# The last down-projection tile in parts of 384 and 128 tokens in place of two of 256

## What is computed

```
x = x + 0.5 * swiglu(rms_norm(x, ffn1_norm), ffn1_gate, ffn1_up, ffn1_down)
x = x + hybrid_mixer(rms_norm(x, mix_norm), w_in, ...)
x = x + 0.5 * swiglu(rms_norm(x, ffn2_norm), ffn2_gate, ffn2_up, ffn2_down)
return rms_norm(x, final_norm)      # x * rsqrt(mean(x * x) + eps) * gain

swiglu(h) = (silu(h @ w_gate) * (h @ w_up)) @ w_down      # hidden width 2816
```

## Time and profile before

| | us |
|---|---|
| median of 3 runs | 976.95 |
| lowest and highest | 974.39 and 976.98 |
| the profiled execution | 975.18 |
| its span (first to last record) | 973.4 |
| PE busy in the span | 950.9 (98%) |
| DVE, ACT, POOL busy | 675.0, 434.2, 352.4 |

### The profile page before, as it was taken

How to read it: one execution, slowest core, us unless ns; L and a number is a source line. 1 busy time by engine, 2 the same in 40 slices (tenths; PEclk the granted TensorE clock), 3 DMA queues, 4 the chain that set the end, 5 groups by cost and what they waited for, 6 DMA issues and landing times.

```text
span 973.4 us, 16526 instructions
## 1 busy us (share of the span) xinstructions
PE 950.9 (98%) x6290; PEld 848.3 (87%) x6290; DVE 675.0 (69%) x956; ACT 434.2 (45%) x684; POOL 352.4 (36%) x241
## 2 busy tenths in 40 slices
PE   9999999999999999999998999999999999999997
PEld 8789999998888887777898788889999999888887
DVE  6599999997543374676576864369989998753444
ACT  7555454545522223554442323454554555543331
POOL 0866767671011153110100005286676767000001
PEclk9999999999999999999998999999999999999999
DMA  6323333332222335122211123232323232222222
GB/s 206 133 85 109 108 111 105 109 106 79 80 101 91 102 93 173 51 73 75 83 42 44 44 87 106 89 130 82 113 89 126 90 125 86 87 88 85 98 98 87
DMA packets 31101, 94.22 MB, mean 97 GB/s; under 512 B 4464, under 2 KB 7712, under 8 KB 31056
## 3 DMA queue, kind: packets, MB, share of 16 engines
q1 hardware_dynamic: 29120, 90.28, 28.3%
q0 software_dynamic: 1648, 3.07, 1.2%
q10 hardware_dynamic: 288, 0.26, 0.1%
HBM read 90.38 MB, written 2.42 MB: 95 GB/s over the span
## 4 chain that ended last, share of the span: by engine, by line
PE 82%; DVE 6%; ACT 3%; issue 1%; POOL 0%; DVEq 0%; ACTq 0%; POOLq 0%
PE ps L566 26%; PE ps L568 25%; PE ps L567 25%; DVE w_lo L1466 2%; PE ps L833 1%; ACT w_hi L1087 1%; PE ps L854 1%; PE ps L913 1%; DVE s_lo L1517 1%; PE ps L886 1%; DVE h_lo L1613 1%; ACT h L1095 1%; PE ps L843 0%; PE ps L946 0%; DVE odiff L1866 0%
## 5 line engine op out<-in xcount | busy, mean ns | idle before, releaser
L1466 DVE TENSOR_TENSOR w_lo<-raw,w_hi 128x1024 fp32r<-128x1024 f32 (+2 forms) x128 | 186.0, 1453 | 160.0 <-ACT w_hi L1087 159.9
L1087 ACT ACTIVATE w_hi<-raw 128x1024 fp32r<-128x1024 f32 (+2 forms) x128 | 131.3, 1026 | 202.9 <-PE ps L568 202.5
L566 PE MATMUL ps<-xg_hi,w_hi 128*128 128x256 f32 (+1 forms) x528 | 179.5, 340 | 4.8 <-DVE w_lo L1466 2.4
L568 PE MATMUL ps<-xg_hi,w_lo 128*128 128x256 f32 (+1 forms) x528 | 176.0, 333 | 0.0
L567 PE MATMUL ps<-xg_lo,w_hi 128*128 128x256 f32 (+1 forms) x528 | 175.8, 333 | 0.0
L566 PE MATMUL ps<-s_hi,sum_hi 128*128 128x256 f32 x576 | 159.8, 277 | 1.8 <-ACT snap L1182 1.7
L567 PE MATMUL ps<-s_lo,sum_hi 128*128 128x256 f32 x576 | 159.3, 277 | 0.0
L568 PE MATMUL ps<-s_hi,sum_lo 128*128 128x256 f32 x576 | 159.1, 276 | 0.0
L567 PE MATMUL ps<-h_lo,w_hi 128*128 128x512 f32 x330 | 128.4, 389 | 0.0
L566 PEld LDWEIGHTS ps<-xg_hi,w_hi 128*128 128x128 f32 x528 | 100.5, 190 | 24.3 <-issue 14.3
L566 PEld LDWEIGHTS ps<-s_hi,sum_hi 128*128 128x128 f32 x576 | 108.3, 188 | 2.5 <-issue 2.5
(11 more groups left out here) (254 smaller groups left out, 1899.5 us busy)
## 6 DMA issues: line engine op xcount, KB each, us to landing
raw<-up_w SPq DMA_DIRECT2D x50, 512.0 KB, 4.2
raw<-down_w SPq DMA_DIRECT2D x38, 512.0 KB, 3.2
raw_u<-up_w SPq DMA_DIRECT2D x36, 512.0 KB, 3.3
raw<-t_w SPq DMA_DIRECT2D x15, 512.0 KB, 3.3
raw<-out_w SPq DMA_DIRECT2D x8, 512.0 KB, 3.3
raw<-nat_w SPq DMA_DIRECT2D x4, 576.0 KB, 3.7
x<-xT SPq DMA_DIRECT2D x8, 256.0 KB, 4.8
out<-x SPq DMA_DIRECT2D x8, 256.0 KB, 2.2
```

What stands on the lines that cost most here:

```text
L566: pe.matmul(out_ap, a[0], b[0], start=first, stop=False, skip_group_check=resumed)
L568: return pe.matmul(out_ap, a[1], b[0], start=False, stop=last, skip_group_check=resumed)
L1087: act.activation(dst, raw[:, slot(s), 0:w], ACT.Copy).then_inc(hi_ready, 1)
L1466: dve.tensor_tensor(lo, raw[:, slot(s), 0:w], hi, ALU.subtract).then_inc(lo_ready, 1)
```

## The change

The last tile's first part takes tokens 0 to 383 (three blocks of 128) and its second part tokens 384 to 511 (one block). All that belongs to a part follows: the matmuls' width, the factor, the add, the square, the gain, the number of sums, diagonals and spreads (3 and 1 in place of 2 and 2), the multiplications by POOL and DVE and the stores (four DMAs of 2x384 tokens, four of 2x128). The sums for c = 0 use banks 2 to 4 in place of 2 and 3. The places on PE move to kk = 9 (sums for c = 0), 20 (its spread) and 21 (first sum for c = 1).

```diff
-LAST_MEAN, LAST_SPREAD, LAST_SUM = 4, 12, 15
+LAST_MEAN, LAST_SPREAD, LAST_SUM = 9, 20, 21
...
-def half_blocks(c):
-    return range(c * NB // 2, (c + 1) * NB // 2)
+def last_blocks(c):
+    return range(NB - 1) if c == 0 else range(NB - 1, NB)
+
+
+def last_tokens(c):
+    return slice(last_blocks(c)[0] * P, (last_blocks(c)[-1] + 1) * P)
...
-            t = half_tokens(0)
+            t = last_tokens(0)
             pool.wait_ge(rinv_ready, 4)
             pool.wait_ge(xgain_ready, KT - 1)
             for k in range(KT):
...
-                    t = half_tokens(c)
+                    t = last_tokens(c)
                     for kk in range(FT):
...
-                        last = three(ps[:, HALF_BANK[c], 0:HALF], (last_hi[:, kk, :], last_lo[:, kk, :]),
+                        last = three(ps[:, HALF_BANK[c], 0:len(last_blocks(c)) * P], (last_hi[:, kk, :], last_lo[:, kk, :]),
                                      (h_hi[kk][:, t], h_lo[:, kk, t]), kk == 0, kk == FT - 1)
...
-                t = half_tokens(c)
+                t = last_tokens(c)
                 dve.wait_ge(last_done, c + 1)
-                dve.scalar_tensor_tensor(gate_s[:, 0, t], ps[:, HALF_BANK[c], 0:HALF], 0.5, rinv[:, t],
+                dve.scalar_tensor_tensor(gate_s[:, 0, t], ps[:, HALF_BANK[c], 0:len(last_blocks(c)) * P], 0.5, rinv[:, t],
                                          ALU.mult, ALU.mult).then_inc(down_scaled, 1)
```

More of the change, by code:

```diff
@@ L444, in _ @@
                         sp.wait_ge(final_ready, all_dve + k + 2)
-                    sp.dma_start(out[k:k + 2, :, half_tokens(c)].rearrange("k p s -> p k s"),
-                                 x[:, k:k + 2, half_tokens(c)]).then_inc(out_stored, 16)
+                    sp.dma_start(out[k:k + 2, :, last_tokens(c)].rearrange("k p s -> p k s"),
+                                 x[:, k:k + 2, last_tokens(c)]).then_inc(out_stored, 16)
             sp.wait_ge(out_stored, 16 * KT)
@@ L765, in first_mean_squares @@
                     pe.wait_ge(rms_ready, 4)
-                for i, b in enumerate(half_blocks(c)):
+                for i, b in enumerate(last_blocks(c)):
                     pe.matmul(ps[:, MEAN_BANK + i, c:c + 1], sq_sum[:, b * P:(b + 1) * P], ones[:, 0:1],
@@ L782, in last_spread_rms @@
                 pe.wait_ge(diag_ready, 4 + c)
-                for b in half_blocks(c):
+                for b in last_blocks(c):
                     last = pe.matmul(ps[:, LAST_STAT[c], b * P:(b + 1) * P], ones[:], rinv[:, b * P:(b + 1) * P],
@@ L1105, in last_square @@
             def last_square(c):
-                t, bank = half_tokens(c), LAST_STAT[c]
+                t, bank = last_tokens(c), LAST_STAT[c]
                 act.wait_ge(x_updated, 3 * KT + c)
@@ L1114, in last_square @@
                 act.wait_ge(stat_ready, 7 + 2 * c)
-                b = slice(half_blocks(c)[0], half_blocks(c)[-1] + 1)
-                act.activation(rnat[:, b], ps[:, MEAN_BANK:MEAN_BANK + 2, c], ACT.Sqrt, bias=eps_t[:])\
+                b = slice(last_blocks(c)[0], last_blocks(c)[-1] + 1)
+                act.activation(rnat[:, b], ps[:, MEAN_BANK:MEAN_BANK + len(last_blocks(c)), c], ACT.Sqrt, bias=eps_t[:])\
                     .then_inc(rms_ready, 1)
```

## The result

The changed kernel takes 983.6 us, the median of four runs (981.97 to 984.59), against 976.07 (974.39 to 976.98) for the kernel before. The ratio is 1.0078, with a 95% interval of 1.0056 to 1.0099: slower by 7.5 us. The forecast was 980.8, slower by 4.6 to 4.7. The sign was right, and so were the three pieces it was added up from; the loss is 1.6 times as large as forecast, because TensorE's granted clock fell, which the forecast does not have.

A forecast was written before the change was run, and what follows sets the result against it. PE bounds the kernel up to its last product, then a chain through DVE's second factor and the tail. Factor +6.4, tail -1.7, store -0.1 give +4.6 us, set on the mean 976.1: 980.8 us, 8-in-10 range 977.8 to 988.0.

The forecast's parts named there:

- Piece 1: Last tile's products on PE: part one's steps grow to 0.173 us, starting part two 3.5 us later; part two's take 0.115.
- Rivals A: Part two's products: loads hide behind 128 columns, a product costs 0.067 us, total 977.8 us; chance 0.10.
- B: Part two's products: a narrow rounded product costs as much as float32, 0.23 us, total 987.6 us; chance 0.15.
- Piece 2: DVE's queue: three early tiles of c = 0 take 3.1 us ahead of the second factor, which comes 6.4 us late.
- rival C: DVE and POOL don't hinder each other: early tiles take 1.4 us, not 3.1, total 978.6 us; chance 0.05.
- Piece 3: Tail from second factor through DVE's last tiles, at 128 columns: 4.85 us in place of 6.55, a gain of 1.7.

The follow-up runs named there:

- early spread: Changed kernel with the spread for c = 0 at kk = 14 and the sum for c = 1 at kk = 16, not 20 and 21: 981.35 us, ratio 1.0054.
- POOL out of the way: Changed kernel with POOL multiplying only the first column of its three tiles of c = 0, the rest stored unscaled: 981.47 us in one execution.
- both edits: Changed kernel with 256 columns streamed in part two, spread at kk = 14 and sum for c = 1 at kk = 16: 978.27 us, ratio 1.0028.

## Why the prediction was right, and where its sizes were off

The forecast's terms, from T, against the trace of the changed kernel:

| step | forecast | measured |
|---|---|---|
| part one, 66 products of 384 | 11.44 | 11.47 |
| 27 products of 128 | 3.10 | 2.96 |
| sums for c = 0, 12 records | 1.38 | 1.31 |
| 33 products of 128 | 3.80 | 4.59 |
| spread to DVE's early tiles | 1.39 | 2.15 |
| early tiles beside POOL | 3.1 | 3.01 |
| second factor to DVE's last tile | 4.85 | 6.11 |
| last store | 2.6 | 2.71 |
| from T to the end | 31.7 | 34.3 |

**Piece 1** held in what it rested on. Behind 128 columns the step is that of the loads, 0.111 a product against 0.115 taken from the loads of sums, so halving part two saved nearly nothing and the wider part one cost its full 3.5 us. Rivals A (0.067) and B (0.23) are both out; the 0.21 after 964.3 is near B's price, but comes with the granted clock at 0.50. No run has a product that keeps its weights, so that the floor is the load and not something else that each product pays is argued from the loads' own rows, and not tested alone. The Trainium skill's figures for 128 columns ("TensorE: Matmul & The Clock Gate", section "Back-to-back issue gap"), 56 ns isolated and 81 ns in a stream with loads, do not hold for these products of a 4-byte type; the trace has 111.

The terms that were too small go back to the sentence "I take 0.115 for every load in part two", and with it "The keep-warm matmuls ... lie beside it". Both go by the full clock. It fell at 964.3, and three terms carry it: 0.8 in the products, 0.8 in the spread, 1.3 in the tail, 2.8 us together against a miss of 2.6. The kernel with 256 columns streamed and nothing else changed takes this back: 2.3 us after paying 0.6 for longer steps, with the spread to the early tiles back at 1.39 and the tail at 4.9. The prediction has no row of the clock and no rival in which it falls; it asks only what a halved part would cost in time, not what it would do to the engine's rate.

**Piece 2** held: 3.01 us of early tiles against 3.1, released by ACT's copy, and the factor behind them, 2.0 us after the product was ready (2.7 forecast). The kernel before with only the late spread pays 1.4 us for it, and at the full clock the early spread gives 2.2 us back; rival C fell with the two prices measured with POOL out of the way. Which of the two causes shows depends on the other: with the spread early and the clock at half, the factor waits for PE; with the clock full and the spread late, for DVE. The early spread alone brings the factor back by 0.5 us, the full clock alone by 1.1, both together by 3.2.

**Piece 3** had the right gain at full clock: 4.9 us, as forecast, in all three kernels that kept it.

**The range.** That 983.6 lies in 977.8 to 988.0 is in part luck. The forecast's own band was 978.5 to 983.5, and the time is just above it; the range reached further only for rival B, whose mechanism is not what happened.

**The base.** The sum was set on 976.1 and the median is 976.07. The profiled execution of the changed kernel is its fastest of four; the others have a lower mean clock (0.984 to 0.986 of the span against 0.988), so the loss in the median, 7.5, is somewhat larger than the 7.3 from T.

What stays open is what decides the moment of the fall: it came 7.0, 6.7, 5.4, 5.4 and 4.6 us after the first narrow product in the five kernels whose whole second part is narrow, with one trace of each. It may not come in every execution: the fastest of the early spread, 979.05 us, has a mean clock of 0.993 where the other three have 0.985 to 0.989, and no trace of it was kept. No version here beats the kernel before; the best with parts of 384 and 128, with both edits, is 0.28% slower.

## What to carry to other kernels

A matmul that loads its own weights has a floor: here 0.111 us for 128 weight columns of a 4-byte type, with 128 tokens streamed as with one (12 records of sums in 1.31 us). So 256 tokens (0.120) are nearly the narrowest part that pays for itself; at 0.053 for 128 tokens the two meet near 235, an estimate. Below that, making the last part shorter shortens only what comes behind it. Before an uneven split, add up what the longer first part adds ahead of the last one (3.5 us) against what the short tail gives back (1.6 to 1.7). When a step is placed between another engine's work, look at what stands behind its consumer in that consumer's queue: the spread was in time for its own data and still late for DVE.

## What was not expected of the hardware

TensorE's granted clock fell from 1.00 to 0.50 while its records show it busy without a gap. What ran before the fall was a stream of products of 128 columns, 0.111 apart, with 12 records of sums in it; the same stream with 256 columns at 0.120 kept 1.00 until PE was done, through 3.00 us in which PE stood idle, and so did one with only its last 24 products narrow. After the fall products step by 0.213 and plain float32 records by 0.20 to 0.23. In the kernel with the early spread the clock was back up at the end: its second run of keep-warm records took 1.14 us for eight, as at the full clock, where the changed kernel's took 2.05:

```profile
971.03 2.44 PE L783 MATMUL ps<-ones 128*128 128x128 f32 x10
973.26 0.33 PE L777 MATMUL ps<-ones,sq 128*128 128x1 f32 x2
973.46 1.14 PE L783 MATMUL ps<-ones 128*128 128x128 f32 x8
```

So busy time in a profile does not tell that the clock will hold; the row of granted clock has to be read beside it.
